# Row products of a sparse expert layer moved in VectorE's order: more of them between the steps of one search, fewer in the next, later marks two to four up

## The reference

```python
q = (ht @ w_q).reshape(T, PEER_HEADS, PEER_QDIM)
s1 = einsum('thd,nd->thn', q[..., :128], sub_k1)      # 8 heads x 128 key scores, two sets
s2 = einsum('thd,nd->thn', q[..., 128:], sub_k2)
v1, i1 = top_k(s1, 16);  v2, i2 = top_k(s2, 16)
cand = v1[..., :, None] + v2[..., None, :]             # sums of the best scores
vals, pos = top_k(cand, 16)
experts = take(i1 * 128 + i2, pos);  gates = softmax(vals)
a = einsum('cd,chkd->chk', x, expert_u[experts])
out = einsum('chk,chkd->cd', gelu(a) * gates, expert_v[experts])
```

## Time and profile before

| what | us |
|---|---|
| median of 3 runs | 1746.03 |
| lowest and highest of the three | 1743.43, 1749.26 |
| the profiled execution | 1749.67 |
| its span from the first to the last instruction | 1747.9 |

### The profile page before, as it was taken

The page is one execution under the profiler, slowest core; times in us unless marked ns, Lnnn a source line. Parts: engine busy times, 40 slices in busy tenths (PEclk is TensorE's granted clock), DMA queues, the critical chain, the costliest instruction groups (busy, mean ns, idle before and its releaser), DMA issues.

```text
span 1747.9 us, 29485 instructions
## 1 busy us (share of the span) xinstructions
PE 1721.6 (98%) x11745; PEld 1470.2 (84%) x11745; DVE 1096.3 (63%) x2430; ACT 240.9 (14%) x600; POOL 310.4 (18%) x282
## 2 busy tenths in 40 slices
PE   8999999999999999999999999999999999999997
PEld 7887576986999999999999858699955978699953
DVE  4653524797557888899432442379974762379974
ACT  1016510111423111000000011111100001011100
POOL 0010000344324344445322200000000000000000
PEclk9999999999999999999999999999999999999999
DMA  7534243699999999999999645365444535355451
GB/s 280 191 122 169 73 145 121 243 354 384 413 417 415 416 414 399 410 411 416 416 417 418 255 204 191 116 222 169 169 168 169 169 124 191 119 169 169 169 172 69
DMA packets 76609, 439.64 MB, mean 252 GB/s; under 512 B 8566, under 2 KB 8656, under 8 KB 37840
## 3 DMA queue, kind: packets, MB, share of 16 engines
q1 hardware_dynamic: 42624, 305.15, 46.6%
q0 software_dynamic: 32592, 125.92, 18.4%
q10 hardware_dynamic: 1280, 6.96, 1.0%
HBM read 432.69 MB, written 5.24 MB: 251 GB/s over the span
## 4 chain that ended last, share of the span: by engine, by line
PE 81%; DMA 8%; DVE 7%; issue 3%; ACT 0%; POOL 0%; SPq 0%; DVEq 0%; POOLq 0%
PE ps L1156 16%; PE ps L942 14%; PE ps L549 10%; PE ps L934 9%; PE ps L595 7%; DMA arena<-u_rows,sparse_pairs 6%; PE ps L1194 4%; PE ps L634 3%; PE ps L507 3%; DVE arena L1932 2%; PE ps L795 2%; PE ps L844 2%; PE ps L808 2%; PE ps L955 1%; PE ps L1025 1%
## 5 line engine op out<-in xcount | busy, mean ns | idle before, releaser
L934 PE MATMUL ps<-xT,ring 128*128 128x150 f32 x2048 | 266.8, 292 | 0.5 <-ACT arena L1443 0.5
L942 PE MATMUL ps<-arena,ring 128*128 128x150 f32 (+1 forms) x2048 | 266.3, 292 | 0.9 <-DMA ring<-stream 0.9
L934 PEld LDWEIGHTS ps<-xT,ring 128*128 128x128 f32 x2048 | 262.5, 190 | 0.8 <-ACT arena L1443 0.7
L942 PEld LDWEIGHTS ps<-arena,ring 128*128 128x128 f32 x2048 | 262.2, 190 | 1.1 <-issue 1.1
L549 PE MATMUL ps<-ring,arena 128*128 128x512 f32 x416 | 181.4, 592 | 0.4 <-ACT arena L1507 0.4
L2063 DVE SCALAR_TENSOR_TENSOR arena<-arena,sparse_dots 128x1024 f32<-128x1024 f32 x105 | 134.7, 1283 | 72.6 <-DMA arena<-v_rows,sparse_pairs 66.6
L1932 DVE CUSTOM_DVE_ANT_0 arena<-arena 128x1024 f32<-128x1024 f32 x107 | 128.1, 1222 | 73.6 <-DMA arena<-u_rows,sparse_pairs 73.2
L2538 POOL DMA_INDIRECT arena<-v_rows,sparse_pairs x107 | 133.7, 1249 | 224.7 <-DVE arena L2063 182.8
L2501 POOL TENSOR_SCALAR stat<-stat 128x1 f32<-128x1 f32 (+2 forms) x23 | 4.4, 192 | 895.0 <-DVE stat L2237 694.8
L2538 POOL DMA_INDIRECT arena<-u_rows,sparse_pairs x107 | 131.3, 1227 | 163.8 <-DVE sparse_dots L1932 139.6
L549 PEld LDWEIGHTS ps<-ring,arena 128*128 128x128 f32 x416 | 78.0, 190 | 93.0 <-issue 92.3
(11 more groups left out here) (345 smaller groups left out, 2203.3 us busy)
## 6 DMA issues: line engine op xcount, KB each, us to landing
ring<-stream SPq DMA_DIRECT2D x288, 1024.0 KB, 7.7
arena<-second_params POOLq DMA_DIRECT2D x6, 1024.0 KB, 5.3
arena<-kv_scratch POOLq DMA_DIRECT2D x2, 2048.0 KB, 14.0
kv_scratch<-arena ACTq DMA_DIRECT2D x2, 1024.0 KB, 10.8
arena<-held_params ACTq DMA_DIRECT2D x1, 2048.0 KB, 16.6
arena<-u_rows,sparse_pairs POOLq DMA_INDIRECT x107, 15.6
arena<-v_rows,sparse_pairs POOLq DMA_INDIRECT x107, 13.4
arena<-second_params POOLq DMA_DIRECT2D x1, 1536.0 KB, 6.5
```

Of the source, the lines that this page charges most:

```text
L934: ins = pe.matmul(ps[:, o % 2, 0:DENSE], w[:, (o % 2) * D + k * P:(o % 2) * D + (k + 1) * P], xT[:, k, 0:DENSE], start=(k == 0), stop=(k = ...
L942: ins = pe.matmul(ps[:, 4 + k // 2, c:c + DENSE], w[:, (o % 2) * D + k * P:(o % 2) * D + (k + 1) * P], H[:, n, :], start=first and k % 2 = ...
```

## The change

Ten constants change, two tuples of five among them; no instruction is added or removed, and no data differ.

```diff
-DOTS_SCORES = (5, 5, 5, 4, 4)
+DOTS_SCORES = (6, 6, 6, 6, 6)
 DOTS_GATES = DOTS_EARLY + sum(DOTS_SCORES)
-DOTS_SUMS = (4, 4, 4, 4, 3)
-DOTS_PICK = 3
-DOTS_FIRST = 73
-DOTS_TURN = 77
-TURNS_UP = 119
-TURNS_DOWN = 167
+DOTS_SUMS = (2, 2, 2, 2, 2)
+DOTS_PICK = 2
+DOTS_FIRST = 76
+DOTS_TURN = 79
+TURNS_UP = 122
+TURNS_DOWN = 171
 GATES_AT = 22
 WEIGH_AT = 8
-WEIGH_GROUP = 7
+WEIGH_GROUP = 5
```

## The result

| | median, us | lowest and highest | runs |
|---|---|---|---|
| before | 1745.12 | 1742.79, 1749.85 | 20 |
| after | 1749.03 | 1745.81, 1757.12 | 20 |

The ratio is 1.0024, with a 95% interval of 1.0013 to 1.0035. The change costs 0.24%, 3.9 us by the medians. The forecast was 1748.7, so the time came out as forecast. The way there did not.

The account below looks back on a forecast made before the run. It took TensorE, 98% busy, and full DMA engines delivering rows as the bounds. Terms -2.46 - 0.46 + 3.05 + 1.0 + 0.1 + 1.5 gave +2.7 us, so 1746.03 became 1748.7 us; range 1743.2 to 1753.5.

Parts of the forecast that it names:

- Two of its own signs of being wrong: Product 76 starting before 559 without a TensorE wait; second-half gate waits (L955) above 3 us, or none.
- The third: Sign of overall failure: rows 66 to 76 faster than every 3 us without a standstill, or TensorE waiting for the ring.
- The gap at L974: Ahead of tile 0's second transposes: TensorE's wait for the gates goes, -2.46 us.
- the exponentials: Before the transposes: TensorE's loss from ScalarE starting late, as VectorE had not shifted the gates, goes, -0.46 us.
- The casts (+3.05): Before the mixed stage, L2080: row 76 lands at 561.8, so TensorE waits 3.05 us for the selection.
- group 0 (+1.0): Start of the mixed stage: one_hots end later after the casts than the first block, another 1.0 us of wait.
- Group 1 (+0.1): Mixed stage, 81 products instead of 79 before group 1's one_hots: ready at 575.8 against gates at 575.65, 0.1 us.
- The clock (0 in the forecast): From 430 to 840 the granted clock is 1.00, the 2.4 GHz level, so it plays no part.
- The weighing (0, at worst 0.3): Group 5, WEIGH_GROUP 5: VectorE's wait for ScalarE's gelu is just covered, 0, at worst 0.3 us.
- The later marks (+1.5, rival up to 4.4): Second half, three to four rows more asked for: 1.5 us; rival, nothing won back, group 14 waits 4.4, chance 0.2.

Follow-up runs that it names:

- two repeats: The kernel before, unchanged, profiled two more times: 1745.07 and 1746.30 us.
- the marks alone: Changed kernel with the searches' product counts set back as before, keeping 76, 79, 122, 171 and WEIGH_GROUP 5: ratio 1.0024 to the kernel before.
- the old searches with low marks: Kernel before with DOTS_FIRST 70 instead of 73 and DOTS_TURN 73 instead of 77: ratio 1.0003 to the kernel before.
- DOTS_TURN back: Changed kernel with DOTS_TURN 77 instead of 79, all else as changed: ratio 1.0011 to the kernel before.
- early marks down and the rest as changed: Changed kernel with DOTS_FIRST 70 instead of 76 and DOTS_TURN 73 instead of 79: ratio 1.0019 to the kernel before.
- the kernel with all marks low: Changed kernel with DOTS_FIRST 70, DOTS_TURN 73, TURNS_UP 119, TURNS_DOWN 167 and WEIGH_GROUP 7: ratio 0.9992 to the kernel before.
- the searches alone: Changed kernel with DOTS_FIRST 73, DOTS_TURN 77, TURNS_UP 119, TURNS_DOWN 167 and WEIGH_GROUP 7 as before: ratio 1.0008 to the kernel before.

## Why the number was right and the working wrong

The number was met by luck. The forecast took 2.92 us of gain and 5.65 us of cost, +2.7. Against a usual execution of the kernel before the gain is not there, and the cost is 4.9 to 5.2 us, nearly all of it at a place that the forecast had at 0.1. Two of its own signs of being wrong came: product 76 started before 559, at 552.65, with no wait of TensorE for the casts, and no gates waited in the second half. The third did not: from product 69, which waited for its row at 531.0, to 76 the rows came 3.1 us apart, where the limit was 3.

**The gap at L974 and the exponentials (-2.92 us).** In the profiled pair both went, as forecast. In the other profiles with the old order up to there (two repeats, the marks alone, the old searches with low marks) neither is there. The failed step is the one that made the sum against the profiled execution and carried it to the median by taking off 3.6 us: those 3.6 us were largely these waits, so they were taken off twice. Of the 4.6 us between that execution and its first repeat (1749.67 and 1745.07), 2.92 are the two waits and 1.4 TensorE's later arrival at L974 (543.60 less 0.46, against 541.74). An execution 3.6 us above the median of its own kernel was the sign that something in it was not usual. What held is the mechanism: in four executions rows were late (below), and the one with the old searches waited 2.46 us, the three with the new ones not at all.

**The casts (+3.05) and group 0 (+1.0).** Neither came in either profile of the changed kernel. The principle held, that product n is done when fetch n has landed, and that the order does not move rows. Mis-sized was the time of row 76. Row 73 came 210.3 us behind the first dot (544.2 - 333.9), where the execution of the forecast had 215.4; and rows 73 to 76 came 2.83 us apart (544.2 to 552.7) instead of the 3.37 that the forecast put there. Together that is 6.7 us: 218.8 against 561.8 - 336.3 = 225.5. That rows come faster while TensorE stands still, as the forecast had it, is not refuted: from product 73 to 78 it is 2.08 us a row in the execution with the standstill, and 2.88 (545.8 to 560.2) in the first repeat, without one. In the execution of the kernel with DOTS_TURN back, with late rows like the one forecast from, product 76 started at 561.8, as forecast, and TensorE waited 3.37 us. The price was right for late rows.

**Group 1 (+0.1).** This is where the change pays: 3.17 and 2.86 us in two profiles. The forecast had its own numbers for it: row 81 at 571.5, and with 1.2 and 3.1 us behind it 575.8, while TensorE without its wait at L974 would ask at 571.5. It let the late casts cover that, and when the casts were not late, it was bare.

**The clock (0 in the forecast).** "The clock plays no part" was read from an execution in which the idle 2.46 us had no echo. In the changed kernel the echo is 1.66 us, a third of the loss at group 1. The Trainium skill, "TensorE: Matmul & The Clock Gate", section "What's actually happening", says of a kernel's start that the same kernel can show different numbers of matmuls at the low clock from run to run. Of mid-kernel that sentence does not speak; there the profiles here show the like, with and without a fall behind 2.28 to 2.51 us of idle time.

**The weighing (0, at worst 0.3).** It cost 0.17 us in the changed kernel, inside the forecast.

**The later marks (+1.5, rival up to 4.4).** In the changed kernel they cost nothing: no wait in the second half. But this is no proof that they are free. In the 4.83 us lost at group 1 the stream goes on (415 GB/s from 568.5 to 571.7); at that rate they are 2.0 MB or 3.8 rows, an estimate, as many as the later marks ask for. Take the early loss away and the later marks lose 3.0 us themselves, and the weighing 0.9 (one execution of the run with early marks down and the rest as changed). The two overdraw the same stream and **do not add up**: against the kernel with all marks low (0.9992) the later marks and the weighing alone cost 0.27% (1.0019), and the 4.83 us would be 0.28% more, but all of the marks together cost 0.32% (1.0024), each difference with some 0.15% either way. What the early marks cost without the later ones was not run. The forecast, which weighed them as separate terms, had the mechanism and a size inside its bounds, but summed what comes in the other's place.

**What differs between executions, and what stays unsettled.** Two things move against each other. TensorE's arrival at L974 goes by the falls of its clock ahead of it. It came at 539.5 to 540.2 us in the five profiles without a fall, at 541.1 to 541.7 in the six with one fall, at 88 or at 230 us, and at 542.8 to 543.6 in the three with two falls or a longer one (the execution before the change and the one with the wait for the casts had the longer one, from 88 to 95 us). The rows go their own way. In four profiles (before, the searches alone, DOTS_TURN back, and early marks down with the later ones up) product 36 started 89.3 to 93.5 us behind the first dot, in the other ten 83.0 to 85.7. These are the executions with late rows. They have both orders, and two of them (the searches alone and the last) have no fall of the clock ahead. What holds the rows up there is open. And the old order had little spare at L974: tile 0's gates were ready 1.9 us ahead of the eight transposes in the first repeat, 0.4 us in the second and 0.5 in the marks alone, and in the old searches with low marks TensorE met them with nothing to spare (1.16 us for its eight instead of 1.04).

## What to carry to other kernels

A short wait in one profiled execution is not a property of the kernel until a second profile shows it; here two of three executions of the kernel before had no gap to close. Where a stream is full, count how many of its pieces stand ahead of each step that the bounding engine waits for and how much is spare there, at every such step; pieces moved up are paid at the first step without spare time, and later ones may then look free. Price a wait of TensorE with the echo in its clock, here 1.5 to 2.8 us behind ten of the twelve waits of 2.28 us and more from 540 us on.

## What was not expected of the hardware

The clock fell without any idle time in the trace as well. From 88 to 92 us, in work that the change does not touch, behind 32 matmuls of 24 columns and with PE busy 4.00 of 4.00 us here and in the 4 us before, seven of the fourteen profiles show a granted clock of 0.51 to 0.59 (0.52 in the execution before the change) and seven show 1.00. In two of them it lasted on past 92 (0.63 and 0.64 from 92 to 96). The two repeats of before differ in this (1.00 and 0.58), and their times by 1.2 us. Both have another fall from 230 to 234 us (0.60 and 0.75), behind waits of TensorE of 0.4 to 1.3 us that the changed kernel's profile has too, without a fall; and so has the kernel of the old searches with low marks (0.57); the other eleven have none there. So part of the few us by which runs of one kernel differ lies in falls ahead of the stage that the change touches.
